# Compress jobs as float32 column quarters between input jobs, attention steps at two per granule

## What is computed

```python
h = rms_norm(x, ln1_w)
proj = h @ w_in                      # 256 x 2048 @ 2048 x IN_COLS
kc = compress_tokens(k_c, pe_k, w1_k, w2_k)
vc = compress_tokens(v_c, pe_v, w1_v, w2_v)

def compress_tokens(kv, pe, w1, w2): # 15 overlapping blocks of 32 tokens, 2 groups
    blocks = blocks + pe[None, None, :, None, :]
    flat = ...reshape(b, n_cmp, g, CMP_BLOCK * dh)      # 30 rows of 4096
    return jax.nn.gelu(flat @ w1) @ w2                  # w1: 4096 x 256
```

## Time and profile before

| | |
|---|---|
| Median of 3 runs | 2721.87 us (2719.68 to 2726.75) |
| Profiled execution | 2721.16 us, span 2719.5 us |
| PE busy | 2692.3 us (99%) |
| DVE busy | 1839.1 us (68%) |
| ACT busy | 1288.5 us (47%) |
| POOL busy | 88.4 us (3%) |
| DMA | 504.85 MB, 186 GB/s on the mean |
| granted clock of PE, mean | 0.996 |

### The profile page before, as it was taken

One profiled execution on the slowest core, in us unless ns is written; L12 is line 12 of the kernel. 1 busy time (PEld: TensorE's weight loads), 2 busy tenths in 40 slices (PEclk: granted clock), 3 DMA queues, 4 the chain that ended last, 5 costly groups with the idle time before them and its releaser, 6 DMA issues.

```text
span 2719.5 us, 35198 instructions
## 1 busy us (share of the span) xinstructions
PE 2692.3 (99%) x12788; PEld 2230.7 (82%) x12788; DVE 1839.1 (68%) x2404; ACT 1288.5 (47%) x1613; POOL 88.4 (3%) x106
## 2 busy tenths in 40 slices
PE   8999999999999999999999999999999999999998
PEld 7888888788888888888888888888888888888886
DVE  5565767765678567575678766765585966668766
ACT  5564646544454444344445555455363434434342
POOL 1000110100000000000000000000000000000000
PEclk9999999999999999999999999999999999999999
DMA  8765554556676666666666576676565656666663
GB/s 246 241 185 142 155 154 140 160 172 191 226 198 194 195 193 190 194 191 192 193 193 189 191 164 185 188 180 198 184 195 169 197 171 191 199 179 189 179 210 123
DMA packets 261461, 504.85 MB, mean 186 GB/s; under 512 B 16440, under 2 KB 25192, under 8 KB 260288
## 3 DMA queue, kind: packets, MB, share of 16 engines
q1 hardware_dynamic: 256448, 486.73, 59.5%
q0 software_dynamic: 4704, 16.03, 2.6%
q10 hardware_dynamic: 160, 0.04, 0.0%
HBM read 498.66 MB, written 4.08 MB: 185 GB/s over the span
## 4 chain that ended last, share of the span: by engine, by line
PE 97%; ACT 1%; DVE 1%; DMA 0%; issue 0%; ACTq 0%; DVEq 0%
PE acc L294 56%; PE acc L301 28%; PE acc L1904 1%; PE acc L1903 1%; PE acc L1905 1%; PE acc L2033 1%; PE acc L2042 1%; PE mx L508 1%; PE mx L1722 0%; PE mx L341 0%; ACT w_hi L262 0%; PE mx L516 0%; DMA res<-in_x 0%; PE acc L2177 0%; PE acc L2174 0%
## 5 line engine op out<-in xcount | busy, mean ns | idle before, releaser
L270 DVE TENSOR_TENSOR w_lo<-raw,w_hi 128x1024 fp32r<-128x1024 f32 x916 | 1121.4, 1227 | 756.2 <-ACT w_hi L262 739.4
L262 ACT ACTIVATE w_hi<-raw 128x1024 fp32r<-128x1024 f32 x916 | 968.0, 1059 | 1237.1 <-PE acc L301 1148.2
L294 PE MATMUL acc<-w_hi,lt_b_hi 128*128 128x512 f32 x1760 | 685.1, 389 | 0.0
L294 PE MATMUL acc<-w_hi,lt_b_lo 128*128 128x512 f32 x1760 | 684.9, 389 | 0.0
L294 PE MATMUL acc<-w_hi,lt_a_hi 128*128 128x512 f32 x1632 | 638.4, 391 | 0.7 <-DVE lt_b_lo L388 0.7
L294 PE MATMUL acc<-w_hi,lt_a_lo 128*128 128x512 f32 x1632 | 636.9, 390 | 0.0
L301 PE MATMUL acc<-w_lo,lt_b_hi 128*128 128x512 f32 x1760 | 476.8, 393 | 0.0
L301 PE MATMUL acc<-w_lo,lt_a_hi 128*128 128x512 f32 x1632 | 445.7, 395 | 0.9 <-DVE w_lo L270 0.9
L294 PEld LDWEIGHTS acc<-w_hi,lt_b_lo 128*128 128x128 f32 x1760 | 330.4, 188 | 68.8
L294 PEld LDWEIGHTS acc<-w_hi,lt_b_hi 128*128 128x128 f32 x1760 | 330.3, 188 | 68.8
L301 PEld LDWEIGHTS acc<-w_lo,lt_b_hi 128*128 128x128 f32 x1760 | 328.7, 188 | 70.4 <-issue 3.8
(11 more groups left out here) (406 smaller groups left out, 1636.6 us busy)
## 6 DMA issues: line engine op xcount, KB each, us to landing
raw<-in_ret_w_in SPq DMA_DIRECT2D x192, 512.0 KB, 4.1
raw<-in_w_in SPq DMA_DIRECT2D x168, 512.0 KB, 3.7
raw<-in_w_up SPq DMA_DIRECT2D x128, 512.0 KB, 3.8
raw<-in_w_down SPq DMA_DIRECT2D x128, 512.0 KB, 4.7
raw<-in_fox_w_in SPq DMA_DIRECT2D x128, 512.0 KB, 4.4
raw<-in_ret_w_out SPq DMA_DIRECT2D x64, 512.0 KB, 4.2
raw<-in_w_o SPq DMA_DIRECT2D x32, 512.0 KB, 4.4
raw<-in_fox_w_out SPq DMA_DIRECT2D x32, 512.0 KB, 4.6
```

Source lines behind the costliest of these rows:

```text
L262: nc.scalar.activation(w_hi[:, r % 4], raw[:, slot, 2 * half:2 * half + 2, :], ACT.Copy).then_inc(hi_ready, 1)
L270: nc.vector.tensor_tensor(w_lo[:, r % 4], raw[:, slot, 2 * half:2 * half + 2, :], w_hi[:, r % 4].bitcast(F32), ALU.subtract) \
L294: nc.tensor.matmul(acc[par][t][:, :], lt[p][:, kt, t * P:(t + 1) * P], w_hi[:, r % 4, k, :], start=(kt == 0 and p == 0), stop=False)
```

## The change

- The compress jobs become jobs 3 and 5, each between two input jobs (2, 4 and 6); the gdn jobs stay at 7 and later.
- A compress job's 32 products are plain float32, one matmul each, straight from `raw`: no split by ACT and DVE, no `cb`. The blocks are padded to 32 columns and lie in `res`. Product k of a granule writes rows 32k to 32k+31 of one PSUM bank, so the four of a granule stand in four quarters of PE's columns, each with 256 moving columns. PE waits for `raw_loaded` itself.
- ACT copies the 128 x 256 result; the four quarters are added and transposed in step 16 by a matmul with a 0/1 matrix `cmp_sum` (four plain float32 matmuls in place of four transposes), and Gelu moves behind that, to ACT's copy `cmp_hT`.
- The raw places of the job behind a compress job are loaded as that compress job's granules finish on PE (`free=granules_done`), and its first four splits are made ahead of ACT's copy of the compress result. The counters are bumped by nine where a compress job follows.
- The 48 attention steps all lie in jobs 7 to 10: two per granule in jobs 7 and 8 (`DENSE`; PE does one at the start of a granule and one between its matmuls), one in jobs 9 and 10. Compress jobs have no steps.
- SP's loops over input and gdn loads are written out.

```diff
@@ -60,8 +60,9 @@
 J_NSA = 0
-J_CMP = J_NSA + (NH * HD + 6 * NKV * HD) // NB
-J_GDN = J_CMP + 2
+J_IN = (0, 1, 2, 4, 6)
+J_CMP = (3, 5)
+J_GDN = 7
 J_MERGE = J_GDN + 8
...
@@ -229,7 +230,7 @@
-        def load_job(sp, J, src, rows=512, chunks=CPJ):
+        def load_job(sp, J, src, rows=512, chunks=CPJ, free=lo_ready):
...
@@ -237,7 +238,7 @@
-                    wait(sp, lo_ready, J * GPJ + 2 * q + half + 1 - GPJ)
+                    wait(sp, free, J * GPJ + 2 * q + half + 1 - GPJ)
                     sp.dma_start(raw[:, q, 2 * half:2 * half + 2, :].rearrange("p a b -> p (a b)").rearrange(
...
@@ -251,6 +252,12 @@
+        def counted(J, r):
+
+            if not J.terms and any(J.c * GPJ + r + 1 == c * GPJ for c in J_CMP):
+                return 1 + GPJ
+            return 1
+
         def split_hi(act, J, r0, r1):
...
@@ -258,9 +265,10 @@
-                wait(act, granules_done, J * GPJ + r - 3)
+                after_cmp = not J.terms and J.c - 1 in J_CMP and r < 4
+                wait(act, granules_done, J * GPJ + r - 3 - (GPJ if after_cmp else 0))
                 nc.scalar.activation(w_hi[:, r % 4], raw[:, slot, 2 * half:2 * half + 2, :],
-                                     ACT.Copy).then_inc(hi_ready, 1)
+                                     ACT.Copy).then_inc(hi_ready, counted(J, r))
...
@@ -269,12 +277,12 @@
                                         w_hi[:, r % 4].bitcast(F32), ALU.subtract) \
-                    .then_inc(lo_ready, 1)
+                    .then_inc(lo_ready, counted(J, r))
         def ahead(J):
             return GPJ + 4
-        def multiply(pe, J, lt, par, hook=None, mix=None, fresh=None):
+        def multiply(pe, J, lt, par, hook=None, mix=None, fresh=None, dense=1):
...
@@ -286,6 +294,8 @@
                     wait(pe, lt_lo_ready, fresh + r + 1)
+                if dense == 2:
+                    step(mix)
                 wait(pe, hi_ready, J * GPJ + r + 1)
...
@@ -309,11 +319,14 @@
-        def split_job(split, eng, J, mix=None):
-
+        def split_job(split, eng, J, mix=None, dense=1):
+
+            J = lin(J)
             for r in range(GPJ):
-                step(mix)
-                split(eng, J, r + 4, r + 5)
+                for _ in range(dense):
+                    step(mix)
+                if r < 4 or J.terms or J.c + 1 not in J_CMP:
+                    split(eng, J, r + 4, r + 5)
...
@@ -483,8 +495,9 @@
         vc = at(2048 + 662, NKV, HD)
-        cb = [lt.rearrange("p a b -> p (a b)")[:, 0:2 * 960].rearrange("p (v n) -> p v n", v=2)
-              for lt in (lt_b[0][:, :, :], lt_b[1][:, :, :])]
+        blk = [res[:, 0, v * CMP_BLOCK * 32:(v + 1) * CMP_BLOCK * 32].rearrange("p (j n) -> p j n", n=32)
+               for v in range(2)]
+        cmp_sum = at(14512, NKV * NCMP)
         spare = res[:, :, :].rearrange("p a b -> p (a b)")
...
@@ -730,6 +743,7 @@
         NSA_BLOCKS = [2, 0, 1, 3, 4]
+        DENSE = (2, 2, 1, 1)
...
@@ -774,16 +788,16 @@
                 sp.dma_start(dst, src).then_inc(sg("prep_loaded"), 16)
-            with fori(2) as i:
-                for c in range(2):
-                    assert NSA_BLOCKS[1 + c] == c and NSA_BLOCKS[3 + c] == 3 + c
-                    load_job(sp, Lin(1 + c, [(2, i)]), block_of(w_in, 0, i * (3 * NB) + (C_NSA + c * NB)))
-            for c, w in enumerate((w1_k, w1_v)):
-                load_job(sp, J_CMP + c, lambda q, w=w: w[q * 1024:(q + 1) * 1024, :], rows=1024)
-            with fori(2) as g:
-                for kind in range(4):
-                    load_job(sp, Lin(J_GDN + kind, [(4, g)]),
-                             block_of(w_in, 0, g * NB + (C_GDN + kind * NH * HD)))
+            for J in range(1, J_GDN):
+                if J in J_CMP:
+                    w = (w1_k, w1_v)[J_CMP.index(J)]
+                    load_job(sp, J, lambda q, w=w: w[q * 1024:(q + 1) * 1024, :], rows=1024)
+                else:
+                    load_job(sp, J, block_of(w_in, 0, C_NSA + NSA_BLOCKS[J_IN.index(J)] * NB),
+                             free=granules_done if J - 1 in J_CMP else lo_ready)
+            for J in range(J_GDN, J_GDN + 8):
+                g, kind = divmod(J - J_GDN, 4)
+                load_job(sp, J, block_of(w_in, 0, g * NB + (C_GDN + kind * NH * HD)))
             with fori(4) as i:
...
@@ -993,9 +1007,9 @@
-            def copy_job(J, dst, func=ACT.Copy, scale=by_rstd, mix=None):
-
-                split_job(split_hi, act, J, mix)
+            def copy_job(J, dst, func=ACT.Copy, scale=by_rstd, mix=None, dense=1):
+
+                split_job(split_hi, act, J, mix, dense)
                 take(act, J, lin(J).c % 2, lambda t: A(dst(t), acc[lin(J).c % 2][t][:, :], func, scale=scale(t)))
...
@@ -1023,8 +1037,6 @@
                     yield
-                    act.wait_ge(sg("blocks_ready"), kv + 1)
-                    A(cb[0][:, kv, :], blk, ACT.Copy).then_inc(sg("blocks_hi"), 1)
                     yield
...
@@ -1048,8 +1060,17 @@
             mix = blocks_mix()
-            for J in range(1, 5):
-                copy_job(J, lambda t: nat[:, NSA_BLOCKS[J], t, :], mix=mix)
+
+            def hidden(kv):
+                J = J_CMP[kv]
+                wait(act, granules_done, (J + 1) * GPJ)
+                A(cmp_hid[:, kv, :], acc[J % 2][0][:, 0:CMP_HIDDEN], ACT.Copy).then_inc(acc_taken[J % 2], 1)
+
+            for J, blk_ in zip(J_IN[1:], NSA_BLOCKS[1:]):
+                if J - 1 in J_CMP:
+                    split_hi(act, J, 0, 4)
+                    hidden(J_CMP.index(J - 1))
+                copy_job(J, lambda t: nat[:, blk_, t, :], mix=mix)
...
@@ -1068,7 +1089,7 @@
                 act.wait_ge(sg("hid_turned"), 1)
-                A(cmp_hT, mx[:, 0, 0:4 * NKV * NCMP].rearrange("p (a b) -> p a b", a=4), ACT.Copy) \
+                A(cmp_hT, mx[:, 0, 0:4 * NKV * NCMP].rearrange("p (a b) -> p a b", a=4), ACT.Gelu_apprx_tanh) \
                     .then_inc(sg("hid_copied"), 1)
...
@@ -1104,19 +1125,6 @@
             mix = nsa_mix()
-            split_job(split_hi, act, J_CMP, mix)
-            def hidden(kv):
-                par = (J_CMP + kv) % 2
-                wait(act, granules_done, (J_CMP + kv + 1) * GPJ)
-                A(cmp_hid[0:NKV * NCMP, kv, :], acc[par][0][0:NKV * NCMP, 0:CMP_HIDDEN],
-                  ACT.Gelu_apprx_tanh).then_inc(acc_taken[par], 1)
-
-            for r in range(GPJ):
-                step(mix)
-                split_hi(act, J_CMP + 1, r + 4, r + 5)
-                if r == 1:
-                    hidden(0)
-            hidden(1)
...
@@ -1557,48 +1565,44 @@
                 yield
-                pe.wait_ge(acc_taken[0], 1)
+                pe.wait_ge(acc_taken[0], J_IN[0] // 2 + 1)
                 pe.wait_ge(sg("prep_taken"), 1)
                 pe.wait_ge(sg("gates_done"), 1)
                 turn_nsa(0)
                 turn_nsa(1)
                 for _ in range(8):
                     yield
-                pe.wait_ge(acc_taken[1], 1)
+                pe.wait_ge(acc_taken[1], J_IN[1] // 2 + 1)
                 turn_nsa(2)
                 turn_nsa(3)
                 for _ in range(8):
                     yield
-                pe.wait_ge(acc_taken[0], 2)
+                pe.wait_ge(acc_taken[0], J_IN[2] // 2 + 1)
                 turn_nsa(4)
                 turn_nsa(5)
                 for _ in range(8):
                     yield
-                pe.wait_ge(acc_taken[1], 2)
+                pe.wait_ge(acc_taken[0], J_IN[3] // 2 + 1)
                 turn_nsa(6)
+            def multiply_blocks(kv):
+                J, par = J_CMP[kv], J_CMP[kv] % 2
+                pe.wait_ge(acc_taken[par], J // 2)
+                pe.wait_ge(sg("blocks_ready"), kv + 1)
+                for r in range(GPJ):
+                    pe.wait_ge(raw_loaded[r], (J + 1) * 16)
+                    for k in range(4):
+                        last = MM(acc[par][0][32 * k:32 * k + 32, 0:CMP_HIDDEN], blk[kv][:, 4 * r + k, :],
+                                  raw[:, r // 2, 2 * (r % 2) + k // 2, (k % 2) * 256:(k % 2) * 256 + 256],
+                                  start=(r == 0), stop=(r == GPJ - 1))
+                    last.then_inc(granules_done, 1)
+
             mix = blocks_mix()
-            for J in range(1, 5):
-                multiply(pe, J, lt_a, J % 2, mix=mix)
-
-            def multiply_blocks(kv, mix):
-                J, par = J_CMP + kv, (J_CMP + kv) % 2
-                pe.wait_ge(acc_taken[par], J // 2)
-                pe.wait_ge(sg("blocks_lo"), kv + 1)
-                for r in range(GPJ):
-                    pe.wait_ge(lo_ready, J * GPJ + r + 1)
-                    for k in range(4):
-                        if k == 2:
-                            step(mix)
-                        j = 4 * r + k
-                        hi, lo = (w[:, r % 4].rearrange("p a b -> p (a b)")[:, k * 256:(k + 1) * 256]
-                                  for w in (w_hi, w_lo))
```

(44 more changed lines are left out.)

5 lines of the change are left out of this document (2 added, 3 removed).

## The result

The changed kernel takes 2727.4 us (median of 22 runs) where the kernel before takes 2721.8 (22 runs). The ratio is 1.0020, its 95% interval 1.0014 to 1.0026: slower by some 5.6 us, inside the 0.3% that counts as no change here. Two of the 22 executions of the changed kernel took 4540 and 8111 us, with a mean granted clock of 0.56 and 0.33; no other execution of any version did, the ratio goes without them, and nothing here explains them. The profiled execution has 2725.67 us and a span of 2724.0, 4.5 above the 2719.5 of before. The forecast was 2722 with a range of 2714 to 2731.

The account below looks back on a forecast made before the run. TensorE's in-order queue was taken to bound the kernel. Compress jobs -5.85 us (-34.1 + 9.6 + 11.4 + 7.25) and denser steps +5.65 gave -0.2, 2721.0 for the profiled execution, 2722 as median; range 2714 to 2731.

Parts of the forecast that it names:

- PE's work in the compress jobs: Jobs 3 and 5: 64 float32 matmuls at 0.218 us plus 0.25 for going into and out of quarters, 7.25 us a job.
- Rival 4: Compress jobs: all four quarters run side by side, job 5 ends at 3.7, -1.0 us, 2721; chance 0.10.
- The load ahead of job 3: First compress job: DMA is still catching up, so landings feed the job and it takes 11.4 us instead of 7.25.
- 1 KB pieces: Compress weight loads: about 0.17 us more for each 512 KB; job 3 would take 10.1 us if they cost nothing.
- rival 2: The clock falls once or twice more, 1.7 to 3.4 us a fall; with two, 2724 to 2731; chance 0.20.
- The steps that move: Jobs 7 to 10: all 48 steps there, the first 32 two to a granule; waits and extra records sum to 5.65 us.
- step 26: Attention steps in the gdn jobs: PE waits 0.55 us.
- Step 25: Compress probabilities: a wait of 2.7 us if the clock is full, taken as 0 because a clock loss hides it.
- the record term of step 16: Hidden transposes: 4 matmuls (8 records) where 4 transposes were, taken as 0.5 us more.
- Rival 1: Both compress jobs: quarters run one after another, 13.9 instead of 7.0 us a job, 2731.6 us; chance 0.05.
- rival 3: Gdn jobs: the denser steps do not make PE wait, 2717 us; chance 0.13.
- rival 5: Both the waits of the steps and the DMA backlog at job 3 stay away, 2712.7 us; chance 0.08.

Follow-up runs that it names:

- The later place: Changed kernel with the compress jobs as jobs 4 and 6 instead of 3 and 5: 2718.6 us (0.9989).
- fillers: Changed kernel with useless 128 x 512 matmuls on PE, three behind each granule of job 3, five behind job 3, nine behind job 5: 2726.0 us (1.0011).
- spread steps: Changed kernel with the 16 doubled granules spread over the 32 granules of jobs 7 to 10: 2721.1 us (0.9998).

## Why the prediction was right, and where it was not

**PE's work in the compress jobs: wrong in the reading, small in effect.** I took 7.25 us a job from the gram block, because 32 records in 1.08 us seemed to mean that a matmul's second record waits for its first. The gram block's 1.08 is as well 0.87 (two halves side by side) plus the seams, which I had counted as a cost on top. Two quarters take 7.0, four take 3.66. Rival 4 was the case, and its mechanism came as described: job 5 takes 5.80 (3.66 and a wait of 2.14 for job 6's split), not 7.25. I had priced it at -1.0; it gave -1.45, and took 1.7 back through the clock, since PE then waited behind job 5, where I had put no wait.

**The load ahead of job 3: right.** Forecast 11.4 us, measured 11.35, with waits of 3.2 among the granules (forecast 2.5) and 1.45 ahead of job 4 (forecast 1.5). PE started the eighth granule at 95.99 (its landing was forecast for 95.4), ACT the next job's first split at 97.32 (96.7). The later place settles that the backlog is the cause. That the length came out to 0.05 us is luck: its end is set by landings and its start is not, so both were 0.6 to 0.7 late, and the profiles above with the same loads have 10.5 to 11.35. One part was sized wrong: 1 KB pieces cost 0.7 us, not 1.3 (and the two rates that I took it from give 0.20 us for each 512 KB, not 0.17, so 1.6); the backlog itself made up the rest.

**The clock: a rival that came true beside the forecast.** I left the two extra falls at 0.20 as rival 2, at 1.7 to 3.4 us each. They cost 1.5 and 1.7, and this is the largest single difference from the sum. The reason was in my own text: PE idles for 4 us in pieces in job 3. The rival should have been joined to the forecast, since the forecast itself made the idle time. The second fall could not be seen from 7.25 us a job, since then PE does not wait behind job 5; the version with two quarters shows that.

**The steps that move: right in kind, 2 us short.** The waits that I placed at 1.65, 1.2, 1.2, 0.55 and 0.55 were 1.6, 0.9, 1.0, 0.5 and, for step 26, 0.2. Step 25, which I took at nothing and bounded at 2.7, had 0.7 behind the fall of 207 to 214 us; in the two kernels whose falls lay elsewhere (fillers, two quarters) it had 1.8. I missed 0.6 in step 1, for ACT's copy of job 6's result, which the last `turn_nsa` needs. The kernel before has this wait as well, with 0.3: there PE would have been at the step 2.26 us behind the start of its job, here at 1.98 (155.06 less the wait, from 152.53). The waits by name add up to 5.5, and the record term of step 16 was 0.5. Without the clock's loss, jobs 7 to 10 took 135.6 us against 128.0 for the same work before, so 7.6 where my sum had 5.65. Of what is left over those 6.0, the second breaks have 0.6 at most. Another half may lie in how PE gets going behind a wait: with the two table loads gone, waits of 1.9 us went and 2.4 us with them. That was not measured by itself.

**The sum.** Job 7 started at 152.53 (forecast near 150) and job 11 at 293.19 (near 289, and wrong from 5 us off). -0.2 us was expected and +4.5 was measured between the profiled executions: jobs 3 to 6 +1.8 (the clock +3.2, job 5 -1.45), jobs 7 to 10 +1.9, the start +0.6, the rest +0.4. The range held because rival 2 was in it; the likeliest value was 5.4 us too low.

**The other rivals.** Rival 1, quarters one after another, would have been 2734.0 us by the kernel with one quarter (forecast for it 2731.6). Rivals 3 and 5, without the waits of the steps and, in 5, without the backlog, were not the case, but can be had: spread steps gave 2721.1 (2717 by rival 3), and with the later jobs 2711.3 (2712.7 by rival 5).

**What stays open.** Behind a wait of 1.95 to 2.5 us for the split behind a compress job the clock fell in seven places and stayed full in one; behind the thin matmuls in one piece it fell in 18 of 22. What decides it, these runs do not show, nor why the scatter behind job 11 is as large as it is. It was not tried to keep the clock full in job 3 with fillers short enough for its waits.

## What to carry to other kernels

A job that is made shorter on the bound engine hands its end to whatever feeds it: look up, at the place where it will stand, how far the DMA queue is behind, and put it where the queue has caught up (here 22 us later, for 8.8 us). If steps must go denser, spread the doubled places so that each chain PE, DVE, ACT, PE has its time, rather than doubling a stretch; a layout of the three queues from profiled durations found a pattern that gave, by the estimate above, 5.7 us of the 7.5 it promised. And count the idle time that a forecast itself creates as a cost of the clock too, and look for work that can fill it.

## What the hardware showed that I had not expected

- Four plain float32 matmuls of 32 stationary columns in four column quarters start 6 to 7 ns apart; the first record of all four goes first, then the second of all four, 0.22 us later. 64 records: 3.66 us in four quarters, 7.0 in two, 13.9 in one.
- Job 3 with PE busy for 6.67 of 11.35 us, between landings, brings the granted clock to 0.50 for some 10 us (also in the versions with spread steps and without Gelu); the same stretch with fillers or one quarter (PE busy throughout), or with two (7.95 of 11.16 us), stays at 1.00.
- In or right behind 3.6 us of matmuls with 7 and 15 columns or rows, PE busy throughout, the granted clock went to 0.50 in 18 of 22 cases; cut in two with a full granule's matmuls between, in none of eight halves.
- A table load on ACT took 1.28 us, twice, with no more than 0.02 us of gap at either side.
